# A hybrid decoder step on one core: where the transposes of q, k and of the last probabilities stand in TensorE's stream at the end of a head

## What is computed

```
q, k, v, u, ga, gp = jnp.split(h @ w_in, SPLITS, axis=-1)      # h = rms_norm(x), 1024 wide
q = rms_norm(q.reshape(b, t, N_HEADS, 2, HEAD_DIM), q_norm)     # 8 heads, two parts of 64
k = rms_norm(k.reshape(b, t, N_HEADS, 2, HEAD_DIM), k_norm)
s = einsum('bqhcd,bkhcd->bhcqk', q, k) * scale                  # causal
p = softmax(s)[:, :, 0] - lam * softmax(s)[:, :, 1]
o = einsum('bhqk,bkhe->bqhe', p, v)
```

## Time and profile before

| | us |
|---|---|
| median of 3 runs | 2236.02 (2234.69 to 2236.35) |
| the profiled execution, its own time | 2238.14 |
| its span (first to last instruction) | 2236.3 |
| PE busy | 2125.4 (95%) |
| DVE, ACT, POOL busy | 1059.9, 677.9, 505.8 |
| mean granted clock of TensorE | 0.984 of full |

### The profile page before, as it was taken

The page is one execution under the profiler, slowest core; times in us unless marked ns, Lnnn a source line. Parts: engine busy times, 40 slices in busy tenths (PEclk is TensorE's granted clock), DMA queues, the critical chain, the costliest instruction groups (busy, mean ns, idle before and its releaser), DMA issues.

```text
span 2236.3 us, 34616 instructions
## 1 busy us (share of the span) xinstructions
PE 2125.4 (95%) x13557; PEld 1921.8 (86%) x13557; DVE 1059.9 (47%) x1381; ACT 677.9 (30%) x1333; POOL 505.8 (23%) x388
## 2 busy tenths in 40 slices
PE   6999999999999999699899999999999999999998
PEld 6888888888888888598899978889988998899996
DVE  5665565665400101155465343445554555455555
ACT  4444444444443433123303221212211221122120
POOL 5432332332110101142232200212211221122120
PEclk9999999999999999799999999999999999999999
DMA  5122111212277885310222430011111110111112
GB/s 150 50 59 59 38 49 31 58 49 69 75 241 266 283 277 190 116 48 26 62 89 88 143 118 1 30 56 48 41 32 53 48 58 29 40 47 58 30 38 91
DMA packets 176073, 186.30 MB, mean 83 GB/s; under 512 B 8730, under 2 KB 148774, under 8 KB 175917
## 3 DMA queue, kind: packets, MB, share of 16 engines
q1 hardware_dynamic: 165429, 175.21, 25.1%
q10 hardware_dynamic: 10496, 8.92, 1.2%
HBM read 161.09 MB, written 23.24 MB: 82 GB/s over the span
## 4 chain that ended last, share of the span: by engine, by line
PE 87%; issue 4%; DVE 3%; POOL 2%; ACT 2%; DMA 1%; SPq 1%; ACTq 0%; POOLq 0%; DVEq 0%
PE PS L1309 36%; PE PS L1941 12%; PE PS L873 7%; PE PS L268 4%; PE PS L270 4%; PE PS L269 4%; PE PS L1763 3%; PE PS L302 3%; PE PS L326 3%; PE PS L925 3%; PE PS L315 2%; PE PS L940 1%; PE PS L979 1%; SPq L1676 1%; PE PS L281 1%
## 5 line engine op out<-in xcount | busy, mean ns | idle before, releaser
L1296 POOL TENSOR_TENSOR fw_lo<-fw_raw,fw_hi 128x1024 fp32r<-128x1024 f32 (+1 forms) x92 | 218.1, 2371 | 914.9 <-ACT fw_hi L1292 870.4
L1309 PE MATMUL PS<-m_hi,fw_hi 128*128 128x384 f32 (+1 forms) x1032 | 228.4, 329 | 2.3 <-issue 2.3
L1309 PE MATMUL PS<-m_hi,fw_lo 128*128 128x384 f32 (+1 forms) x1032 | 227.6, 328 | 0.4 <-issue 0.4
L1309 PE MATMUL PS<-m_lo,fw_hi 128*128 128x384 f32 (+1 forms) x1032 | 227.5, 328 | 0.0
L268 PE MATMUL PS<-w_hi,act_hi 128*128 128x384 f32 (+1 forms) x576 | 208.9, 363 | 0.0
L2068 DVE TENSOR_TENSOR x<-x,PS 128x512 f32<-128x512 f32 x198 | 136.0, 688 | 139.8 <-PE PS L1941 139.7
L270 PE MATMUL PS<-w_hi,act_lo 128*128 128x384 f32 (+1 forms) x576 | 196.3, 341 | 0.0
L269 PE MATMUL PS<-w_lo,act_hi 128*128 128x384 f32 (+1 forms) x576 | 196.0, 340 | 0.0
L1309 PEld LDWEIGHTS PS<-m_hi,fw_hi 128*128 128x128 f32 x1032 | 175.8, 188 | 3.6 <-POOL fw_lo L1296 1.8
L1309 PEld LDWEIGHTS PS<-m_hi,fw_lo 128*128 128x128 f32 x1032 | 176.3, 188 | 0.7 <-issue 0.7
L1309 PEld LDWEIGHTS PS<-m_lo,fw_hi 128*128 128x128 f32 x1032 | 176.4, 188 | 0.0
(11 more groups left out here) (238 smaller groups left out, 3908.4 us busy)
## 6 DMA issues: line engine op xcount, KB each, us to landing
k_pg<-in_cache_k_dram SPq DMA_DIRECT2D x64, 512.0 KB, 4.8
v_pg<-in_cache_v_dram SPq DMA_DIRECT2D x64, 512.0 KB, 5.4
fw_raw<-in_w_up_dram SPq DMA_DIRECT2D x44, 512.0 KB, 4.1
fw_raw<-in_w_in_dram SPq DMA_DIRECT2D x24, 512.0 KB, 4.6
wd_raw<-in_w_down_dram SPq DMA_DIRECT2D x22, 512.0 KB, 4.2
w_raw<-in_w_in_dram SPq DMA_DIRECT2D x21, 512.0 KB, 5.2
out_dram<-raw SPq DMA_DIRECT2D x16, 512.0 KB, 3.7
ga_scratch<-ga_ring ACTq DMA_DIRECT2D x8, 544.0 KB, 7.1
```

The lines of the kernel that those rows point to most:

```text
L1296: e.tensor_tensor(fw_lo[slot][:, 0:kts, :], fw_raw[:, 0:kts, :], fw_hi[slot][:, 0:kts, :].bitcast(F32), ALU.subtract).then_inc(fw_tail, 1)
L1309: ins = e.matmul(PS[:, 3 * slot + c, 0:cw], w[slot][:, kt, :], x[:, k0 + kt, c0:c0 + cw], start=first and kt == 0, stop=last and kt == kts ...
```

## The change

In step 8 the q transposes move from in front of the 24 matmuls to behind the ninth, and are followed at once by the first group of the head's last probabilities; the second group, which stood behind the matmuls, follows the k transposes behind the fifteenth. In steps 0 to 4 the q transposes (they exist at s = 2) move from in front of the matmuls to behind the first group, ahead of kt = 2. The first scores of a head wait for one release of bank 7 less, that is, not for the last output copy of the head before (L479). ACT's copies in step 8 follow PE's new order.

```diff
         def pe_scores(e, h, slot, s):
             if s == 0:
-                e.wait_ge(b7_free, FIRST_USES + h * USES_PER)
+                e.wait_ge(b7_free, FIRST_USES - 1 + h * USES_PER)
@@ pe_head
+                def first_and_q():
+                    first_group()
+                    q_part()
+
+                def q_and_first():
+                    q_part()
+                    first_group()
+
+                def k_and_second():
+                    k_part()
+                    second_group()
+
                 if s == QT:
-                    q_part()
-                    matmuls({5: k_part})
-                    first_group()
-                    second_group()
+                    matmuls({3: q_and_first, 5: k_and_second})
                 elif s < 5:
-                    q_part()
-                    matmuls({2: first_group, 5: k_part})
+                    matmuls({2: first_and_q, 5: k_part})
                 else:
                     first_group()
                     q_part()
@@ act_head
-                if s == QT:
-                    if group:
-                        act_evac_qk(e, *group)
-                    take_matmuls()
+                if group and s == QT:
+                    act_evac_qk(e, *group, parts=(0,))
                 if s >= 1:
                     act_evac_probs(e, h, s - 1, 0)
                 if group and s < QT:
                     act_evac_qk(e, *group, parts=(0,))
+                if group and s == QT:
+                    act_evac_qk(e, *group, parts=(1,))
                 if s >= 5:
                     act_evac_probs(e, h, s - 1, 1)
                 if s < QT:
                     act_exp(e, h, s)
                 if group and s < QT:
                     act_evac_qk(e, *group, parts=(1,))
-                if s < QT:
-                    take_matmuls()
+                take_matmuls()
```

## The result

The changed kernel took 2216.4 us in the median of four runs (2213.3 to 2217.6) against 2236.2 in the median of four runs of the kernel before: a ratio of 0.990 (95% interval 0.9875 to 0.9928). On a second chip it took 2219.2 against 2238.2, ratio 0.991 (0.990 to 0.9925). The forecast was 2212.6. The whole time alone does not tell the forecast's case from its rival *Clock falls all the same* (2215.8); the profile does.

A forecast was written before the change was run, and what follows sets the result against it. PE was taken as the bound (87% of the chain, 4% issue), stopping where heads end. Savings of 10.6 + 1.5 + 6.1 + 2.0 + 3.2 = 23.4 us from the 2236.0 median gave 2212.6 us, range 2208 to 2222.

The forecast's parts named there:

- the forecast's case: Whole kernel: all priced savings arrive, 23.4 us, and the clock stays at 2.4 GHz behind both branches; 2212.6 us, chance 50%.
- Clock falls all the same: Rival: gaps of 1.3 and 1.9 us behind the branches still lower TensorE's clock; 20.2 us saved, 2215.8 us, chance 20%.
- The end of a head: Step 8 to the next scores, heads 0, 2, 4, 5, 6: 11.23 us becomes 9.11, 2.12 saved each, 10.6 together.
- The covers: Step 8's new order: copies and probabilities finish before PE asks for them, the first group's by half a microsecond.
- Head 7: Its end, without q or k part: 9.53 us before, 7.97 plus 0.1 for just meeting `p_ready` after; 1.5 us saved.
- The branches: Backward branches behind heads 1 and 3: shorter head ends plus earlier branch issue save 3.04 and 3.02 us, together 6.1.
- the last copy ends at 6.53, the branch goes at 6.72: Behind head 1, in us from the 14 value matmuls: branch issued just after ACT's last copy; next scores at 10.6.
- upper bound of 9.4: Most that heads 1 and 3 could save together, in us, with no idle left at the branches.
- Step 2: q behind the first group: wait for E of about 0.45 us replaces POOL's 0.85; 2.0 us saved over five heads.
- The clock behind the branches: Starts of heads 2 and 4: shorter idle keeps TensorE at 2.4 GHz; 3.2 us saved, bounds 0 and 4.1.
- head 0's start: First scores lose a 0.7 us wait, but step 1's scores wait for ACT's exponential behind a weight load; counted as nothing.
- 23.4: Total predicted saving in us: 10.6 + 1.5 + 6.1 + 2.0 + 3.2.

The follow-up runs named there:

- late semaphore: Changed kernel with one more wait, for the projection tile's copy, ahead of the fifth block of a head's last values; ratio to the kernel before 0.9936.
- written-out loop: Changed kernel with TensorE's stage 1 loop over heads 0 to 5 written out, other engines keeping theirs; 2208.3 us, ratio to the kernel before 0.987.
- copies earlier: Changed kernel with the k transposes and second group ahead of kt = 4, not kt = 5, in step 8; one run, 2213.8 us.

## Why the prediction was right, and where it was off

**The end of a head**: 9.11 us forecast, 9.16 measured, 2.07 saved and not 2.12. The covers held: no head waits for E, q, k or a copy in step 8. Pricing by start-to-start distances gave the 0.6 us of draining and filling that a sum of the idle times (1.50) would have left out.

**Head 7**: 1.5 forecast, 1.7 measured. The 0.1 us wait for `p_ready` did not show.

**The branches**: 6.1 forecast for heads 1 and 3; from the 14 value matmuls to the next scores 10.79 us both times, so 2.85 and 3.38 saved, 6.2. The late semaphore and the written-out loop confirm the mechanism. That the sum is so close is luck, since two misses cancel. The first is in "the last copy ends at 6.53, the branch goes at 6.72". It went at 7.0, 0.55 us behind the copy, because the sequencer was as far ahead as it gets; the row of stage 5 with its 18 matmuls was the right measure. The queue of 64 entries in the Trainium skill, TensorE: Matmul & The Clock Gate, section on the array's architecture, would have let it go 0.3 us earlier; this trace does not bear that out. The second miss: the second branch took 3.48 us and not the 4.17 of the profile of before, so the gaps were 1.57 and 1.57 us and not 1.3 and 1.9. The branch is not of one length, and the forecast carried each over as one profile had it. The upper bound of 9.4 is also a slip: with no idle left, 13.64 + 14.17 - 2 x 9.11 = 9.6 us and not 9.4.

**Step 2**: the old wait was replaced by one for E of 0.33 us (0.45 forecast) in heads 1 to 5 and of 0.18 in head 6, heads 2 and 4 among them as forecast. But the saving was 0.3 us in heads 1, 3 and 5 and 0.24 in head 6, not 0.4. The forecast priced both waits by their idle time; at the head's end it had counted what a stop costs beyond that, here it had not. The run with step 2's groups one kt later shows that the wait of 0.33 us costs 0.5.

**The clock behind the branches**: 3.2 forecast with a chance, about 2.7 measured (heads 2 and 4 together 6.85, less 2 x 2.07 for their ends). Step 1's scores came 4.1 us earlier, as priced (6.37 and 7.35 us behind the first ones before, 4.79 and 4.81 now); what was given back at step 2 was 1.4 and not 0.9, the same step sized too small.

**The step that failed** is head 0's start: "I cost that at nothing". The lost wait was indeed worth nothing, since step 1's scores wait for an exponential that stands behind a weight load from DRAM; their wait grew from 1.47 to 2.37 us. But the clock then fell: step 2's scores came 6.93 us behind step 1's and not 5.50. Head 0 saved 0.6 us where my terms give 2.5. That is 1.9 of the 2.8 us by which stage 1 missed 23.4, and it is two things. The first scores stand 7.23 us ahead of step 1's and not 6.32: these 0.9 us are mostly the wait that was taken out ahead of the point from which stage 1 is counted, and no time lost. The other 1.0 us is the clock's fall, less what the slower head no longer waits for at step 2: with the clock up, in the run with the loop written out, head 0 lasted 66.09 us and not 67.13. The rest of the 2.8 is step 2, in the heads above and in heads 2 and 4, and the ends of the heads at 2.0 to 2.1 us and not 2.12. I cannot call the fall an effect of the change: it came in ten of the twelve profiles whose wait there was 1.68 us or more, with and without the first scores' wait ahead of it, and in neither of the two of the kernel before, where it was 1.47 and 1.49.

**Outside stage 1** the changed kernel's first profile lost 1.9 us (1635.2 against 1633.3 from the key pages to the end). All of it lies between the first and the fourth branch of stage 5 (446.5 against 444.6 us), whose lengths vary from one execution to the next; the second profile has 445.3 there. Over the whole of the later stages, the ten profiles with TensorE's loop of stage 1 in place lasted 1629.7 to 1638.0 us and the four with it written out 1628.3 to 1630.3. The forecast's "stages 2 to 5 as long as before" holds within that scatter; nothing here ties the rest of it to the change, and its cause stays open.

## What to carry to other kernels

An engine's loop branch costs only what the instructions already queued ahead of it do not cover, so the last semaphore an iteration waits for decides its price, up to how far the sequencer gets ahead (here 2.2 us of work): move that wait away from the end, or write the loop out if it is short. After either, read the branches of the later loops again: here they went from 3.3 us and more to 0.21 with no edit of theirs. When a wait is hidden, look for the next producer due at the same place, and at the heads that were too slow to wait: they will start to. Parts of a change that cannot be told alone in the whole time (here two of three) can still be measured by the distance between two fixed points of a profile, if the change does not move one of the points and a second profile has shown how far the distance scatters.

## What the runs showed that I had not expected

TensorE's clock did not follow the length of the gap alone. Behind the branch gaps up to 1.75 us (eight in four profiles) it never fell; of 1.81 and 1.78 in one profile the first brought a fall to 0.72 and the other none; of ten gaps between 2.75 and 4.12 us all but one (3.11) brought one, and step 1's scores then came 1.5 to 2.8 us later. A gain from the clock is one to forecast with a chance and not with a number.

The backward branch of stage 1's loop took between 3.3 and 4.75 us in different executions, the exit 0.083; that of stage 5's took 3.3 to 3.8 us, or 0.21 when nothing but code ahead of it had grown. And TensorE's sequencer got no further ahead than about 18 matmuls with their weight loads, in stage 5 as behind heads 1 and 3 in the changed kernel and with the copies earlier.
